# Low parts of the wide feed-forward weights moved from GpSimd to VectorE in a two-part transformer kernel

## What is computed

```python
def swiglu(h, w1, w3, w2):
    return (jax.nn.silu(h @ w1) * (h @ w3)) @ w2

def first_block(...):            # DEPTH = 2
    for i in range(DEPTH):
        sh1, sc1, g1, sh2, sc2, g2 = ada(c, ada_w[i], ada_b[i])
        h_l = rmsnorm(x, norm1_g[i]) * (1 + sc1) + sh1
        ...                      # i = 0: latent attention and a short convolution; i = 1: Fourier mixer
        x = x + g1 * out_l
        x = x + g2 * swiglu(rmsnorm(x, norm2_g[i]) * (1 + sc2) + sh2, ffn_w1[i], ffn_w3[i], ffn_w2[i])
def second_block(...):           # one layer
    x = x + gt1 * parallel_mixer(h, ...)   # window attention beside a linear recurrence
    x = x + gt2 * moe_ffn(h, ...)          # 32 experts, 4 for each token
    return rms_norm(x, g_final)
```

## Time and profile before

| | |
|---|---|
| median of 3 runs | 1897.08 us (1891.97 to 1900.2) |
| time of the profiled execution | 1898.97 us |
| its span, first to last instruction | 1897.2 us |
| TensorE busy | 1692.5 us, 89% |
| VectorE busy | 878.2 us, 46% |
| ScalarE busy | 441.0 us, 23% |
| GpSimd busy | 363.7 us, 19% |
| mean granted TensorE clock | 0.941 |

### The profile page before, as it was taken

How to read it: one execution, slowest core, us unless ns; L and a number is a source line. 1 busy time by engine, 2 the same in 40 slices (tenths; PEclk the granted TensorE clock), 3 DMA queues, 4 the chain that set the end, 5 groups by cost and what they waited for, 6 DMA issues and landing times.

```text
span 1897.2 us, 24286 instructions
## 1 busy us (share of the span) xinstructions
PE 1692.5 (89%) x9444; PEld 1071.0 (56%) x9444; DVE 878.2 (46%) x1175; ACT 441.0 (23%) x679; POOL 363.7 (19%) x119
## 2 busy tenths in 40 slices
PE   6989889999889999786899999999986989799776
PEld 2863579999589999664733444334332433344222
DVE  5767579988549988676321221221121212122012
ACT  3324544443334443454200000000000000000001
POOL 1632035553245553553000000000000000000000
PEclk8998989999999999898799999999998989899988
DMA  8623358886338877443599999999999999999994
GB/s 326 238 88 105 118 211 279 285 282 233 137 141 280 286 277 242 150 178 111 231 403 422 421 422 421 421 422 421 420 421 421 421 421 420 421 415 418 422 421 196
DMA packets 100607, 586.61 MB, mean 309 GB/s; under 512 B 12225, under 2 KB 13505, under 8 KB 45153
## 3 DMA queue, kind: packets, MB, share of 16 engines
q1 hardware_dynamic: 100512, 585.35, 79.1%
HBM read 584.26 MB, written 1.05 MB: 309 GB/s over the span
## 4 chain that ended last, share of the span: by engine, by line
PE 57%; DVE 19%; DMA 16%; issue 4%; SPq 3%; ACT 2%; DVEq 0%; ACTq 0%
PE psum L1032 21%; PE psum L1048 10%; DVE accl L1617 7%; DMA araw<-ada_dram 7%; DMA mraw<-dn_dram 4%; PE psum L611 3%; PE psum L1008 3%; PE psum L612 3%; PE psum L613 3%; SPq L398 2%; DMA mraw<-gu_dram 2%; PE psum L1061 2%; DVE accl L1616 2%; DMA mlast<-gu_dram 1%; DVE work L1672 1%
## 5 line engine op out<-in xcount | busy, mean ns | idle before, releaser
L1552 POOL TENSOR_TENSOR wl<-raw,wh 128x1024 fp32r<-128x1024 f32 (+1 forms) x100 | 353.9, 3549 | 510.5 <-ACT wh L1160 291.1
L1032 PE MATMUL psum<-mraw,xsat 128*64 128x512 f32 (+2 forms) x1648 | 413.6, 640 | 40.0 <-DMA mraw<-gu_dram 26.5
L1032 PEld LDWEIGHTS psum<-mraw,xsat 128*64 128x64 f32 (+2 forms) x1648 | 137.3, 143 | 271.5 <-issue 270.5
L1048 PE MATMUL psum<-mraw,xsat 128*64 128x512 f32 (+2 forms) x848 | 208.1, 636 | 12.7 <-DMA mraw<-dn_dram 9.9
L793 PE MATMUL psum<-ah,wh 128*128 128x256 f32 x704 | 203.8, 289 | 15.6 <-DVE al L1676 11.0
L794 PE MATMUL psum<-al,wh 128*128 128x256 f32 x704 | 201.9, 287 | 0.0
L795 PE MATMUL psum<-ah,wl 128*128 128x256 f32 x704 | 201.7, 287 | 0.0
L611 PE MATMUL psum<-ah,wh 128*128 128x256 f32 (+1 forms) x440 | 136.0, 309 | 32.6 <-DVE al L1676 9.5
L1032 PE MATMUL psum<-mlast,xsat 128*64 128x512 f32 (+2 forms) x400 | 146.3, 653 | 16.6 <-DMA mraw<-gu_dram 16.6
L793 PEld LDWEIGHTS psum<-ah,wh 128*128 128x128 f32 x704 | 137.5, 195 | 17.4 <-issue 11.5
L2190 DVE TENSOR_TENSOR oacc<-psum,oacc 128x512 f32<-128x512 f32 x60 | 38.7, 686 | 222.8 <-PE psum L1061 222.8
(11 more groups left out here) (354 smaller groups left out, 2548.0 us busy)
## 6 DMA issues: line engine op xcount, KB each, us to landing
mraw<-gu_dram SPq DMA_DIRECT2D x206, 1024.0 KB, 20.2
mraw<-dn_dram SPq DMA_DIRECT2D x106, 1024.0 KB, 25.5
araw<-ada_dram SPq DMA_DIRECT2D x128, 512.0 KB, 4.5
mlast<-gu_dram SPq DMA_DIRECT2D x50, 1024.0 KB, 21.4
raw<-ffa_dram SPq DMA_DIRECT2D x44, 1024.0 KB, 7.4
raw<-blk_dram SPq DMA_DIRECT2D x56, 512.0 KB, 3.4
raw<-ffb_dram SPq DMA_DIRECT2D x44, 512.0 KB, 5.6
mlast<-dn_dram SPq DMA_DIRECT2D x22, 1024.0 KB, 26.4
```

What stands on the lines that cost most here:

```text
L1032: last = mm(ps[4 + n][a * w:(a + 1) * w, :], xs[:, k * P + a * w:k * P + (a + 1) * w], slots[slot][:, i * 2 * D + n * 512:i * 2 * D + (n + ...
L1048: last = mm(ps[n][a * w:(a + 1) * w, :], at[:, k * P + a * w:k * P + (a + 1) * w], slots[slot][:, i * D + n * 512:i * D + (n + 1) * 512], ...
L1552: sub = lambda o, a, b: nc.gpsimd.tensor_tensor(o, a, b.bitcast(F32), ALU.subtract)
```

## The change

In `ffn(0)` and `ffn(1)` the wide low part is made by VectorE, as two subtractions of 128x1024 (`wide_lo`), between `mul_lo` and the second `ada` of a pass. GpSimd has no work in the loops. Blocks no longer take slot b % 6: a table `SPLIT` gives the slot of `wh` and `wl`, `SPLIT_BEFORE` what must have been multiplied before, and `RAW` moves blocks 21 to 36 to the columns of `raw` from 5120 on, so that they lie beside the wide weights. With this the order changes around each network:

- The first wide weights of a network are loaded, and both parts made, while the last blocks ahead of it are multiplied (`ffn_first`, `last_blocks`, `wide_lo(l, 0, 0)` and `wide_lo(l, 1, 1)`).
- The first three blocks behind a network are loaded and their high parts made at its end, ahead of the square-root table and the squares on ScalarE. One of the three, block 27 or 36, shares columns of `raw` with narrow slot 1 and is called `shared`.
- SyncE loads blocks 21 to 25 and the first weights of network 0 ahead of `ada(28)`, behind a wait for the fourth v product.
- GpSimd waits for `s_h` (norm 2 scaled) before it subtracts block 29, for `s_hl` (norm 4 split) before block 37 and for `s_mnl` (the merged mixer output split) before block 52.

```diff
 NB = 56
-NRAW, NSPLIT = 3, 6
+NRAW = 3
+SPLIT = [b % 6 for b in range(B_O)] + [0, 1, 4, 5, 2, 3, 4, 5] * 2 + [0, 1, 4, 5, 2, 3] * 2 + [0, 1] + [4, 3, 5, 2, 0, 1, 5, 2]
+SPLIT_BEFORE = [max([k + 1 for k in range(b) if SPLIT[k] == SPLIT[b]], default=0) for b in range(NB)]
+RAW = [(5120 if B_O + NRAW <= b < B_2 + NRAW else 0) + (b % NRAW) * D for b in range(NB)]
 WIN = [(0, (0, 1, 2, 3)), (0, (4, 5, 6, 7)), (1, (0, 1)), (1, (2, 3)), (1, (4, 5)), (1, (6, 7))]
...
                     sp.wait_ge(s_lo, b - NRAW + 1)
-                sp.dma_start(raw[:, (b % NRAW) * D:(b % NRAW + 1) * D], blk_d[b]).then_inc(s_raw[b % NRAW], 16)
+                sp.dma_start(raw[:, RAW[b]:RAW[b] + D], blk_d[b]).then_inc(s_raw[b % NRAW], 16)
             def expert_load(i, number=None):
...
             ada(25)
-            for b in range(B_O + NRAW, B_O + NSPLIT):
-                blk(b)
             ada(26)
             ada(27)
-            for b in range(B_O + NSPLIT, B_F):
+            sp.wait_ge(s_v, 4)
+            for b in range(B_O + NRAW, B_F):
                 blk(b)
-            for n in range(28, 48):
-                ada(n)
-
             def ffn_a(l, slot, src):
...
                 sp.dma_start(raw[:, 2 * FA + slot * D:2 * FA + (slot + 1) * D], src).then_inc(s_fbraw[slot], 16)
+            def ffn_first(l):
+                if l == 0:
+                    sp.wait_ge(s_lo, B_O + 2)
+                else:
+                    sp.wait_ge(s_flo, NF)
+                    sp.wait_ge(s_fblo, NF)
+                ffn_a(l, 0, ffna_d[l, 0])
+                ffn_b(l, 0, ffnb_d[l, 0])
+                if l == 0:
+                    sp.wait_ge(s_lo, B_O + NRAW)
+                ffn_a(l, 1, ffna_d[l, 1])
+
             def ffn(l):
-                sp.wait_ge(s_lo, B_F if l == 0 else B_2)
-                if l == 0:
-                    sp.wait_ge(s_v, 4)
-                for f in range(2):
-                    ffn_a(l, f, ffna_d[l, f])
-                    ffn_b(l, f, ffnb_d[l, f])
+                sp.wait_ge(s_lo, B_F - 1 if l == 0 else B_2)
+                ffn_b(l, 1, ffnb_d[l, 1])
                 base_n = 48 + 48 * l
...
                         ffn_b(l, u % 2, ffnb_d[l, bass.ds(f, 1), :, :].rearrange("a p n -> p (a n)"))
+                shared = B_F + 1 if l == 0 else B_2 + 2
+                for b in range(shared - 1, shared + 2) if l == 0 else range(B_2, B_2 + NRAW):
+                    if b != shared:
+                        blk(b)
                 for j in range(6):
                     ada(base_n + 40 + j)
+                sp.wait_ge(s_fblo, (l + 1) * NF)
+                blk(shared)
                 if l == 0:
...
                     sp.dma_start(tabs[:, :, :, :], tab_d).then_inc(s_par, 16)
-                else:
-                    sp.wait_ge(s_flo, 2 * NF)
-                    sp.wait_ge(s_fblo, 2 * NF)
-                    for b in range(B_2, B_2 + NRAW):
-                        blk(b)
                 for j in range(6, 8):
                     ada(base_n + 40 + j)
+            ffn_first(0)
+            for n in range(28, 48):
+                ada(n)
             ffn(0)
-            for b in range(B_F, B_2):
+            for b in range(B_F + NRAW, B_2 - 2):
+                blk(b)
+            ffn_first(1)
+            for b in range(B_2 - 2, B_2):
                 blk(b)
             ffn(1)
+            sp.wait_ge(s_flo, 2 * NF)
             for b in range(B_2 + NRAW, B_V2):
...
                 expert_load(i)
-            sp.wait_ge(s_blk, NB - 3)
+            sp.wait_ge(s_blk, NB - 6)
             for i in range(n0, n1):
...
                 act.wait_ge(s_raw[b % NRAW], 16 * (b // NRAW + 1))
-                wait(act, s_blk, b - NSPLIT + 1)
-                A(wh[:, (b % NSPLIT) * D:(b % NSPLIT + 1) * D], raw[:, (b % NRAW) * D:(b % NRAW + 1) * D], ACT.Copy
-                  ).then_inc(s_hi, 1)
+                wait(act, s_blk, SPLIT_BEFORE[b])
+                A(wh[:, SPLIT[b] * D:(SPLIT[b] + 1) * D], raw[:, RAW[b]:RAW[b] + D], ACT.Copy).then_inc(s_hi, 1)
             def load_table(function):
...
             A(ah3[:, 3, 0:T], ps[1][:, 0:T], ACT.Copy).then_inc(s_ao, 1)
-            for b in range(B_O + NSPLIT, B_F):
-                block_hi(b)
-
-            def x_by_blocks(b):
-                return lambda j: act.wait_ge(s_ev, b + j + 1)
-
-            def x_by_ffn(k):
-                return lambda j: act.wait_ge(s_x, DJ * k + j + 1)
             def ffn_hi(l, slot, loaded):
...
                 A(wh[:, w], raw[:, w], ACT.Copy).then_inc(s_fhi, 1)
+
+            def last_blocks(l, end):
+                act.wait_ge(s_blk, end - 6)
+                ffn_hi(l, 0, 16)
+                block_hi(end - 2)
+                block_hi(end - 1)
+                act.wait_ge(s_blk, end - 2)
+                ffn_hi(l, 1, 16)
+
+            last_blocks(0, B_F)
+
+            def x_by_blocks(b):
+                return lambda j: act.wait_ge(s_ev, b + j + 1)
+
+            def x_by_ffn(k):
+                return lambda j: act.wait_ge(s_x, DJ * k + j + 1)
             def ffn(l):
...
                         down_hi(NF - 1, (NF - 1) % 2, 16 * ((NF - 1) // 2 + 1))
+                next_block = B_F if l == 0 else B_2
+                act.wait_ge(s_fgu, (l + 1) * NF - 1)
+                block_hi(next_block)
+                block_hi(next_block + 1)
+                act.wait_ge(s_fdn, (l + 1) * NF)
+                block_hi(next_block + 2)
             norm_squares(1, x_by_blocks(B_O))
...
             act.wait_ge(s_blk, B_F)
-            ffn_hi(0, 0, 16)
             h_hi(1, 3)
-            ffn_hi(0, 1, 16)
             ffn(0)
...
             act.wait_ge(s_fdn, 1 + NF)
-            for b in range(B_F, B_F + NRAW):
+            for b in range(B_F + NRAW, B_2 - 2):
                 block_hi(b)
...
                 A(ah3[:, c, 0:T], ps[c % 2][:, 0:T], ACT.Copy).then_inc(s_f2h, 1)
-                if c in (2, 4, 6):
-                    block_hi(B_F + NRAW + c // 2 - 1)
-            for b in range(B_F + NSPLIT, B_2):
-                block_hi(b)
+            last_blocks(1, B_2)
             norm_squares(3, x_by_blocks(B_F))
...
             h_hi(3, 9)
-            ffn_hi(1, 1, 16)
             ffn(1)
...
             act.wait_ge(s_fdn, 1 + 2 * NF)
-            block_hi(B_2)
             norm_root(4)
-            for b in range(B_2 + 1, B_2 + NRAW):
-                block_hi(b)
             h_hi(4, 12)
-            for b in range(B_2 + NRAW, B_2 + NSPLIT):
+            for b in range(B_2 + NRAW, B_2 + 6):
                 block_hi(b)
...
             A(lam[:, 1, :], lam[:, 0, :], ACT.Exp, scale=-1.0).then_inc(s_lru, 1)
-            for b in range(B_2 + NSPLIT, B_XG):
+            for b in range(B_2 + 6, B_XG):
                 block_hi(b)
...
                 pool.wait_ge(s_hi, b + 1)
-                s = slice((b % NSPLIT) * D, (b % NSPLIT + 1) * D)
-                sub(wl[:, s], raw[:, (b % NRAW) * D:(b % NRAW + 1) * D], wh[:, s]).then_inc(s_lo, 1)
-
-            def ffn(l):
-                def lo(f, fv):
-                    wait(pool, s_fhi, f + (l * NF + 1))
-                    s = slice((fv % 2) * FA, (fv % 2 + 1) * FA)
-                    sub(wl[:, s], raw[:, s], wh[:, s]).then_inc(s_flo, 1)
-
-                lo(0, 0)
-                lo(1, 1)
-                with pool.Fori(0, (NF - 2) // 4) as i:
-                    f0 = pool.snap(i * 4)
-                    for u in range(4):
-                        lo(f0 + (2 + u), u)
-
-            for b in range(B_F):
+                s = slice(SPLIT[b] * D, (SPLIT[b] + 1) * D)
+                sub(wl[:, s], raw[:, RAW[b]:RAW[b] + D], wh[:, s]).then_inc(s_lo, 1)
+
+            for b in range(B_F + NRAW):
                 block_lo(b)
-            ffn(0)
-            for b in range(B_F, B_2):
+            pool.wait_ge(s_h, 3 * DJ)
+            for b in range(B_F + NRAW, B_2):
                 block_lo(b)
-            ffn(1)
+            for b in range(B_2, B_2 + NRAW):
+                block_lo(b)
             pool.wait_ge(s_fml, 2 * NF)
...
                 nc.gpsimd.tensor_tensor(g_, g_, x_, ALU.mult).then_inc(s_gel, 1)
-            for b in range(B_2, NB):
+            pool.wait_ge(s_hl, 4 * DJ)
+            for b in range(B_2 + NRAW, NB):
                 if B_OUT2 <= b < B_OUT2 + 4:
                     gelu_arg(b - B_OUT2)
+                if b == B_OUT2 + 4:
+                    pool.wait_ge(s_mnl, 8)
                 block_lo(b)
...
                         TTn(al3[:, k, T:2 * T], work[:, k, T:2 * T], f32(ah3[:, k, T:2 * T]), ALU.subtract).then_inc(s_hlx, 1)
+
+            def wide_lo(l, f, fv):
+                wait(dve, s_fhi, f + (l * NF + 1))
+                for half in range(2):
+                    w = slice((fv % 2) * FA + half * D, (fv % 2) * FA + (half + 1) * D)
+                    ins = TTn(wl[:, w], raw[:, w], f32(wh[:, w]), ALU.subtract)
+                ins.then_inc(s_flo, 1)
             def residual(b, j, g):
...
                     ada(41 + j)
```

(7 more changed lines are left out.)

16 lines of the change are left out of this document (7 added, 9 removed).

## The result

The changed kernel takes 1876.05 us (median of 4 runs, 1874.61 to 1877.88) against 1896.83 of the kernel before beside it; the ratio is 0.9883, with a 95% interval of 0.9863 to 0.9903, a gain of 20.8 us. The forecast was 1873, range 1862 to 1888.

What follows compares the result with a forecast made beforehand. In the networks TensorE waits for VectorE's ml, late because GpSimd's subtraction blocks VectorE's steps. Terms -23.9 - 8.7 + 5.5 + 2 + 3.5 - 3.0 = -24.6 us from 1898.97 give 1874.4, or 1873 us on the median; range 1862 to 1888.

Steps and rivals of the forecast that it cites:

- Passes and second product: Network loops: TensorE's waits for ml close, -23.9 us; second wide product no longer waits 2.24 and 2.19 us for GpSimd.
- the 1 us put down to the clock: Network loops: about 1 us a network stays lost to TensorE's slower clock at the start.
- The 7.1 us of VectorE work a pass: Network passes: VectorE's new work sums to 7.1 us against TensorE's 8.64, so VectorE stops setting the pace.
- Ahead of network 0: Norm before network 0: three scalings fall from 5.55 to 1.27 us without GpSimd's wide subtraction, -4.3 us.
- Behind the networks: Network ends: ScalarE's squares wait for the late shared load; net +5.5 us behind network 0, +2 behind network 1.
- the 1 us for the slower clock at each end: Behind the networks: allowance for TensorE's clock; behind network 1, 1 us on top of a norm 6.7 us late.
- the norm left unblocked: Behind network 0: GpSimd's block subtractions no longer run into the norm, giving back 3.2 us.
- Attention: Attention stage: ada(28) lands late behind earlier loads, and one short VectorE instruction is blocked; +3.5 us, between 0 and +8.
- Recurrence: Four scans: two of three block subtractions leave their time; -3.0 us, between 0 and -3.3.
- the dear waits (2): Rival: new waits cost +17 us at the network ends and +8 in attention; about 1886.5 us, chance 0.15.
- The ring over ScalarE (3): Rival: passes bound by wide load, ScalarE's high part and VectorE's steps; slower than before, 1909 us, chance 0.05.
- That `ml` is late for another reason (4): Rival, network passes: ScalarE's high part mh, not blocking, delays ml, so no gain; about 1897 us, chance 0.03.

Runs made afterwards that it cites:

- e_alone: The kernel before, with only the wide low parts moved to VectorE, the first two pairs beside the norms; loads, high parts and buffers unchanged: 1869.86 us, ratio 0.9851.
- e_back: The changed kernel, with the loops' wide low parts made by GpSimd again, one subtraction of 2048 columns a pass: 1909.8 us, ratio 1.0057.
- e_read: The changed kernel, plus an unused GpSimd subtraction of 2048 columns, reading and writing SBUF, in each pass of the loops: 1937.02 us, ratio 1.0215.
- e_write: The changed kernel, plus two unused GpSimd clears of 2048 columns, which write SBUF and read nothing, in each pass: 1876.08 us, ratio 0.9882.
- e_queue: The changed kernel, with the shared block's load behind two of the six ada loads in SyncE's queue, not behind all six: 1862.3 us, ratio 0.9811.
- e_read1: The changed kernel, plus an unused GpSimd multiplication by a constant, reading one operand of 2048 columns, in each pass: 1891.19 us, ratio 0.9957.

## Why the prediction was right

By the stages of the table, against its own terms:

- **Passes and second product**: predicted -23.9 and, of the -8.7, 2.2 for each second product, together -28.3. Measured -14.6 and -15.1, so -29.8. From the second wide product on, each network takes 184.4 us, at the low end of the predicted 184 to 186; these 1536 matmuls lost none of the 1 us put down to the clock. The slow clock lies ahead of them, where the first 48 matmuls take 8.05 and 8.76 us, at a granted clock of 0.59 and 0.50 in their first 4 us. e_alone shows that the loops need nothing else of the change, and e_back, e_read and e_write the reason given: VectorE waits while GpSimd reads. The 7.1 us of VectorE work a pass were 6.8.
- **Ahead of network 0**: -4.3 predicted for the scalings. From the norm's sums to the first product it took 12.1 us before and takes 7.8 now, so -4.3. The last blocks, beside which the two low parts were to cost nothing, take 0.9 longer; a step of `ada` there took 3.51 us beside GpSimd's low parts of the last two blocks (250.95, in GpSimd's 247.95 to 253.38), and TensorE waited 0.6 us for a residual there.
- **Behind the networks**: +5.5 and +2 predicted, +5.9 and +1.6 measured. The way there was right (load at 463.67, landing 4.97 against 5.2, squares 9.3 us later than before against 10). One term inside it was mis-sized: the 1 us for the slower clock at each end, which no run shows. The 16 sums alone took 3.0 more behind network 0, 6.72 us against 3.72, and 2.3 more behind network 1 (750.36 to 756.40, against 3.72). Two others made up for it: the sums began 6.9 us later than before where the norm was reckoned 7.7 late, and the norm left unblocked was worth 3.9 us (21.0 to 17.1 between the two Fourier products) against 3.2. That the net came out within half a us is luck: in the changed kernel's second trace the sums took 1.5 us more than before and the stage grew by 3.6.
- **Attention**: +3.5 predicted, +5.9 measured, inside the bounds of 0 to +8. The load of `ada(28)` was there at 188.6, not 187, and later steps were late too: steps of `ada` waited 6.7 us for loads from 180 us on, where they waited 2.1, and ScalarE's exponentials stood behind them. Nine traces with this order spread by 4 us in this stage, more than the error.
- **Recurrence**: -3.0 predicted, -2.2 measured, though the four scans gave 3.3 (5.78 to 2.44 us).
- **Not predicted**: +1.0 in the output blocks of the third mixer, +0.3 ahead of network 1, -2.5 in the experts; the last goes with the clock.

The sum of the spans is -23.0 us for -24.6 forecast, and the medians fell by 20.8, and by 23.4 when both kernels ran again. Part of this nearness is cancelling: the networks and the experts gave 4 us more than forecast, the other stages together 5.5 us less.

Of the rivals, the dear waits (2) came true in part, in the attention stage and the clock. The granted clock was 0.53 and 0.70 over the sums behind the pause and 1.00 without it (e_queue), so what the pause cost was not the same in two executions of one kernel. The ring over ScalarE (3) did not come: no pass is longer than TensorE's own 8.64 us, and ScalarE's waits for wide weights in the networks fell from 39.6 us to 2.3, though these landed in 7.7 us by the median for 7.4. (The passes of the kernel before took 9.25 us, not the 9.1 that this rival reckoned with.) That `ml` is late for another reason (4) is refuted by e_alone, e_write and e_read. At 459 each of the two engines waited for the other: the step issued first made GpSimd wait 0.6 us, the next step waited 2.0 for GpSimd.

## What to carry to other kernels

Here the work moved off GpSimd was worth what its reads of SBUF cost VectorE, not its own busy time: its 4.6 us of reading in each pass held VectorE (a step took 4.95 us for 1.27), and 3.7 us of writing in each pass cost nothing (e_write, 0 us). On another kernel, ask what the instruction that is to be moved holds up. When work is put ahead of a stage's end, follow the one load it needs back through its queue, for here a single load behind six others cost 14 us, and moving it ahead of four of them gave them back. And run the core of a change alone: here it was at least as fast as the whole. A stage that follows a long pause of TensorE should be traced twice before a us or two of it is explained: here the same 16 matmuls took 6.72 us in one execution and 5.20 in another.

## What the runs showed of the hardware

- GpSimd's subtraction of 2048 columns took 4.62 us by the median from two tensors and 3.60 in place with one tensor as both inputs (e_read); a multiplication by a constant 1.90 to 2.88, 2.42 by the median (e_read1); a clear of 2048 columns 1.81 (e_write).
- A VectorE step with one tensor input (`TENSOR_SCALAR`, 0.74 us for 1024 columns) took 3.44 us beside GpSimd's reads in e_read, where one with two took 4.18 for 1.27: both were blocked.
- The sums of a norm, 16 matmuls, took 3.72 us at a granted clock of 1.00 (e_queue). Behind a wait of 6.8 us they took 6.72 us in one execution of the changed kernel and 5.20 in another, at granted clocks of 0.53 and 0.70.
